# Nineteen identity products on TensorE and five row scalings moved to GpSimd, in the opening of a two-layer kernel

## What is computed

```
mod = silu(c) @ w_ada + b_ada
shift, scale, gate = split(mod, 3)
h = x * rsqrt(mean(x*x) + eps) * norm_gain * (1 + scale) + shift
proj = h @ w_in
```

## Time and profile before

| | us |
|---|---|
| three runs | 1460.65, 1461.0, 1461.27 |
| profiled execution, its time | 1461.91 |
| its span in the trace | 1460.2 |
| TensorE busy | 1436.3 |
| VectorE busy | 741.5 |
| ScalarE busy | 601.3 |
| GpSimd busy | 112.4 |
| mean granted clock of TensorE, share of full | 0.995 |

### The profile page before, as it was taken

The page is one execution under the profiler, slowest core; times in us unless marked ns, Lnnn a source line. Parts: engine busy times, 40 slices in busy tenths (PEclk is TensorE's granted clock), DMA queues, the critical chain, the costliest instruction groups (busy, mean ns, idle before and its releaser), DMA issues.

```text
span 1460.2 us, 18290 instructions
## 1 busy us (share of the span) xinstructions
PE 1436.3 (98%) x6990; PEld 1207.1 (83%) x6990; DVE 741.5 (51%) x1200; ACT 601.3 (41%) x1009; POOL 112.4 (8%) x131
## 2 busy tenths in 40 slices
PE   6999999999999999999999999999999999999998
PEld 5788879998888888888888888888888888888887
DVE  6741677855665533556455444453457333333332
ACT  5633577755343332333333444532355333333221
POOL 5302322210000000000000111100000000000000
PEclk9999999999999999999999999999999999999999
DMA  9995200123433333312223233344332333333321
GB/s 283 322 237 186 75 1 2 31 73 93 152 101 109 98 97 101 101 44 87 68 63 87 58 87 101 87 144 113 89 90 84 115 89 101 99 93 94 110 79 57
DMA packets 227825, 149.71 MB, mean 103 GB/s; under 512 B 5330, under 2 KB 216014, under 8 KB 227108
## 3 DMA queue, kind: packets, MB, share of 16 engines
q1 hardware_dynamic: 223588, 131.63, 31.2%
q0 software_dynamic: 4160, 17.04, 4.0%
HBM read 140.92 MB, written 6.68 MB: 101 GB/s over the span
## 4 chain that ended last, share of the span: by engine, by line
PE 95%; SPq 1%; DMA 1%; DVE 1%; ACT 1%; issue 1%; DVEq 0%; ACTq 0%
PE ps L433 70%; PE ps L2215 6%; PE ps L2241 3%; PE ps L1938 3%; PE ps L2140 3%; PE ps L1830 3%; PE ps L2227 1%; DMA w_raw<-in_w_in_dram 1%; PE ps L1961 1%; PE ps L1899 1%; PE ps L2126 1%; PE ps L2125 1%; SPq L547 1%; PE ps L1954 1%; SPq L577 0%
## 5 line engine op out<-in xcount | busy, mean ns | idle before, releaser
L453 DVE TENSOR_TENSOR w_lo<-w_raw,w_hi 128x1024 fp32r<-128x1024 f32 (+1 forms) x214 | 258.1, 1209 | 251.0 <-ACT w_hi L448 248.1
L448 ACT ACTIVATE w_hi<-w_raw 128x1024 fp32r<-128x1024 f32 (+1 forms) x214 | 219.4, 1034 | 15.3 <-PE ps L433 11.3
L499 ACT ACTIVATE temps<-ps 128x512 f32<-128x512 f32 x67 | 40.0, 597 | 238.9 <-PE ps L433 238.9
L433 PE MATMUL ps<-g_hi,w_hi 128*128 128x512 f32 x384 | 95.8, 392 | 0.0
L433 PE MATMUL ps<-g_hi,w_lo 128*128 128x512 f32 x384 | 94.9, 389 | 0.0
L433 PE MATMUL ps<-g_lo,w_hi 128*128 128x512 f32 x384 | 94.8, 389 | 0.0
L433 PEld LDWEIGHTS ps<-g_hi,w_lo 128*128 128x128 f32 x384 | 72.1, 188 | 15.0
L433 PEld LDWEIGHTS ps<-g_lo,w_hi 128*128 128x128 f32 x384 | 72.1, 188 | 14.9
L433 PEld LDWEIGHTS ps<-g_hi,w_hi 128*128 128x128 f32 x384 | 71.5, 188 | 14.6
L433 PE MATMUL ps<-f_lo,w_hi 128*128 128x512 f32 x288 | 71.1, 389 | 0.0
L433 PE MATMUL ps<-f_hi,w_hi 128*128 128x512 f32 x288 | 71.1, 389 | 0.0
(11 more groups left out here) (442 smaller groups left out, 2734.8 us busy)
## 6 DMA issues: line engine op xcount, KB each, us to landing
w_raw<-in_w_in_dram SPq DMA_DIRECT2D x107, 512.0 KB, 3.9
w_raw<-in_w_ff_gate_dram SPq DMA_DIRECT2D x22, 512.0 KB, 3.8
w_raw<-in_w_ff_up_dram SPq DMA_DIRECT2D x22, 512.0 KB, 3.8
w_ada_shift_scale<-in_w_ada_dram SPq DMA_DIRECT2D x16, 512.0 KB, 7.8
w_raw<-in_w_r_out_dram SPq DMA_DIRECT2D x16, 512.0 KB, 4.5
w_raw<-in_w_ff_down_dram SPq DMA_DIRECT2D x16, 512.0 KB, 4.2
w_ada_gate<-in_w_ada_dram SPq DMA_DIRECT2D x4, 1024.0 KB, 10.9
x_spill<-x_t POOLq DMA_DIRECT2D x2, 2048.0 KB, 9.0
```

The costliest lines, as they stand in the source:

```text
L433: mm = pe.matmul(bank, w[:, slot, k], mov[:, at_k], start=first and n == 0 and k == 0, stop=last and n == 2 and k == kts - 1)
L448: act.activation(whi[:, slot, 0:kts], raw[:, slot, 0:kts], ACT.Copy).then_inc(hi_done, 1)
L453: nc.vector.tensor_tensor(wlo[:, slot, 0:kts], raw[:, slot, 0:kts], whi[:, slot, 0:kts].bitcast(F32), ALU.subtract).then_inc(lo_done, 1)
L499: act.activation(dst, ps[:, o % 4], func, scale=scale).then_inc(evac, 1)
```

## The change

Two things change, both in the opening.

TensorE gets `keep_busy(n)`, which issues n products of the 128x128 identity with itself, in fp32, into the first 128 columns of PSUM bank 0. Nothing reads them, and the first GEMM overwrites them. Fourteen stand between `rows_bc` and `mod_sums(0)`, five between `mod_sums(0)` and the GEMM. Ahead of each group TensorE waits for three copies of x, the third of which frees bank 0.

`x_rstd` for k-tiles 3 to 7 leaves VectorE. GpSimd does them, after it has issued the copy of the bias line; each waits until `xr_done` has reached k, so product 3 waits for VectorE's third, and each later one for the one before it on GpSimd.

```diff
+X_DVE = 3
+BUSY_AT = (14, 5)
@@ GpSimd, after the copy of the bias line
+            pool.wait_ge(m["row_done"], 1)
+            pool.wait_ge(m["x_ev"], X_ACT)
+            pool.wait_ge(m["x_ev2"], KT - X_ACT)
+            for k in range(X_DVE, KT):
+                pool.wait_ge(m["xr_done"], k)
+                g.tensor_tensor(x_r[:, k], x_t[:, k], rs_row[:], ALU.mult).then_inc(m["xr_done"], 1)
             pool.wait_ge(m["ada_done"], KT)
             pool.wait_ge(m["hl_done"], KT)
@@ VectorE, in the loop over u
-                if u < KT - 1:
+                if u + 1 < X_DVE:
                     x_rstd(u + 1)
@@ TensorE, ahead of the first GEMM
+            def keep_busy(n):
+                pe.wait_ge(m["x_ev"], 3)
+                for _ in range(n):
+                    pe.matmul(ps[:, 0, 0:P], ident[:], ident[:], start=True, stop=True)
+
             pe.wait_ge(m["x_ev"], 2)
             pe.wait_ge(m["rms_rs"], 1)
             rows_bc(7).then_inc(m["rms_bc"], 1)
+            keep_busy(BUSY_AT[0])
             mod_sums(0)
+            keep_busy(BUSY_AT[1])
```

## The result

The changed kernel takes 1466.8 us (median of six runs, 1465.5 to 1468.6) against 1461.1 for the one before, run beside it (six runs, 1460.7 to 1462.2). The ratio is 1.0039, 95% interval 1.0028 to 1.0049: 5.7 us slower. The forecast was 1462.6 with a range up to 1466.0. The time lies 0.8 us above the range, on the side of the rival called alternation, which the prediction put at 1465.7, between 1464.4 and 1466.8.

The account below looks back on a forecast made before the run. TensorE, busy 98%, was taken to bound the kernel, with a DMA floor at 44.60 us in the opening. Identity products and freed VectorE gave 0, GpSimd's hold on VectorE +1.6 us: median 1462.6 us, range 1459.9 to 1466.0.

Parts of the forecast that it names:

- alternation: Opening: GpSimd products follow every single VectorE operation, all in before 40 us; +4.7, 1465.7 us (1464.4 to 1466.8), chance 0.31.
- The fill: Identity products on TensorE before the first GEMM: cost 0, clock kept at full speed, step 1 near 27.7, end gain 0.
- the case that the prediction listed last among its rivals: Opening: clock falls despite the identity products, steps 0 to 3 unmoved, end as in another case; no chance of its own.
- The floor: TensorE's step u = 4 is held to 44.60 us by a DMA load, so earlier clock gains end at 0.
- The scalings taken from VectorE: Opening: VectorE loses five operations of 0.60 us that TensorE did not wait for; gain 0.
- The price of a product: Each GpSimd product holds off VectorE operations with two SBUF inputs, costing VectorE up to 1.15 us.
- The sum: Whole forecast effect: +1.6 us, from products held to true gaps in VectorE's queue, other terms 0.
- gap order: Opening: GpSimd gets in only at true gaps between VectorE operations, last product near 52 us; +1.6 us, chance 0.36.
- the two signs named as proof of a wrong prediction: Step 4 starting before 44.4 us, or VectorE's rows keeping their lengths beside GpSimd's products.
- The rival's own sum: For alternation: ada_sum(3) whole at 40.9, TensorE idle 5.4 us, +3.4 at step 4, plus 1.3 for one half-clock pass.
- From the trace to the median: Profiled execution with +1.6 would be 1463.5 us; it ran 0.9 above the median, so 1462.6 was forecast.
- the leak: Opening: a load lands earlier because work ahead of it ended earlier, and step 1's 1.2 us survive; 1459.8 us, chance 0.06.

Follow-up runs that it names:

- kernel 1: Changed kernel with all eight scalings back on VectorE, the 19 identity products kept: 1461.21 us, ratio 0.9998 to the kernel before.
- kernel 9: Changed kernel with all eight scalings on VectorE and only two GpSimd products (k-tiles 3 and 4) that nobody reads: 1462.28 us, 1.0007 against the kernel before.
- 4: Changed kernel with all eight scalings on VectorE and five GpSimd memsets, which read nothing, at the products' place: 1460.99 us, 0.9999 against the kernel before.
- 8: Changed kernel with all scalings on VectorE; ScalarE and VectorE split weight tiles of steps 3 to 6 one step later: 1461.02 us, 0.9998 against the kernel before.
- kernel 7: Changed kernel with the scaling of k-tiles 3 to 7 left out altogether, ScalarE reading the unscaled tile: 1461.28 us, 1.0001 against the kernel before.
- kernel 2: Changed kernel without the identity products, scalings of k-tiles 3 to 7 still on GpSimd: 1466.74 us, 1.0039 against the kernel before.
- kernel 10: Changed kernel with VectorE scaling k-tiles 0 to 5 and GpSimd only 6 and 7: 1464.48 us, 1.0024 against the kernel before.
- 3: Changed kernel with all eight scalings on VectorE and five GpSimd products into a tile nobody reads: 1466.06 us, 1.0035 against the kernel before.
- kernel 5: Changed kernel plus 19 more identity products on TensorE in step 2, ahead of the sums that wait for ada_sum(3): 1464.28 us, 1.0022 against the kernel before.
- kernel 6: Changed kernel with each GpSimd product after the first waiting for its step's ada_sum, one product per step: 1462.67 us, 1.0008 against the kernel before.

## Why the prediction was wrong, point by point

- **The fill, right.** 14 products took 3.29 us, 0.235 each instead of the 0.22 read from products of half as many columns, five took 1.36 to their last end, neither reached what follows, and the clock was 1.00. Its cost is 0 and so is its gain (kernel 1). Step 1 stood at 27.67 for 27.7 foretold, which is partly luck: in the other kernels with the fill it began at 27.5 to 29.0. And in kernel 9 the clock fell in spite of the fill, the case that the prediction listed last among its rivals.
- **The floor, right in its effect, incomplete in its place.** In the four kernels without products on GpSimd (1, 4, 7, 8) step 4 started at 44.23 to 44.82, whatever else was done. It is held by two loads in a row (kernel 8), not by one, and its place differs by 0.6 us among these four traces.
- **The scalings taken from VectorE gain nothing, right** (kernel 7).
- **The price of a product, right.** Up to 1.15 was the bound, 1.02 to 1.05 measured, in after and in kernels 2, 9 and 10. That it is GpSimd's read is shown (3 against 4).
- **The order in which the two engines take turns: the step that failed.** The sum took the gap order, in which GpSimd gets in only where VectorE's queue is truly empty. It gets in after every single instruction of VectorE, whose records overlap: last product at 37.6, not 52; six multiply-adds at 6.55. The prediction held against alternation that no row showed such a moment inside a stream. But a row that is missing speaks for neither side. The row that showed GpSimd waiting, 866.35, had it begin when VectorE's read ended, at a time when VectorE had nothing queued behind it: the next `w_lo` came at 868.13. So it couldn't tell the two orders apart, and no row of before stood for the gap order. It was taken at 0.36 against 0.31, and the +1.6 us of the sum rests on it alone; measured were +4.7 in the trace. Neither of the two signs named as proof of a wrong prediction came, since both were signs against the floor and the price; the sign that told was the start of the last product, near 38 for alternation.
- **The rival's own sum** held up in the trace: `ada_sum(3)` whole at 40.47 (40.9 foretold), 4.53 us idle (5.4), and at step 4 +3.4 for the wait and +1.3 for the clock, 4.7 together, where 4.73 was measured. Its parts were off in opposite ways, 3.0 and 1.8, so that the sum fits better than its parts, by luck; kernel 5 confirms the split, with 3.1 and 1.6.
- **From the trace to the median: the smaller error.** The trace accounts for 4.7 us, the medians differ by 5.7. The prediction took 0.9 off because the profiled execution of before stood above its median; that of after stood 0.7 below its own (1466.11 against 1466.83). The six spans of after go from 1463.8 to 1466.2, and the profiled one is at the lower end. What differs between executions of one kernel is seen in part in the last section. That it makes up this last 1.0 us is not shown, since only one execution of each has a trace. (The lower end of the range, 1459.9, lay 0.1 above the 1459.8 of the leak that it was meant to take in; nothing rests on it.)

What the change did, then: nothing at its first part, and at its second it traded 0.60 us of VectorE for 1.02, five times within 7.5 us. Step 4 starts at 44.60 without it, so step 3 may start as late as 39.66 and `ada_sum(3)` be whole as late as 37.57 (4.94 and 2.09 earlier). It was whole at 35.26, which left a cover of 2.3 us; that took up the two products of kernel 9 (37.76) but for 0.2 (0.35 by its step 4). With five it was whole at 40.47, 2.9 too late, and the clock that the first part had kept up fell in a new place for another 1.6 to 2.6.

## What to carry to other kernels

Where work goes from VectorE to GpSimd and GpSimd reads SBUF beside operations of VectorE with two SBUF inputs, price each GpSimd instruction at most of its length on VectorE's queue, at once, and compare that with what VectorE is rid of (1.02 against 0.60 here). Where a chain of products can be spread, one to a step, the loss falls to a quarter (1.2 against 4.7 in the traces of kernel 6 and of after), but nothing is gained. And where a new wait of TensorE appears, ask what the clock does behind it: in kernel 10 the slow passes cost as much as the wait.

## What the runs showed of the hardware

- **Turns.** VectorE, whose queue was never empty, didn't keep GpSimd out: a waiting GpSimd instruction went ahead of the next instruction of VectorE each time. Six multiply-adds took 2.46 us with no product among them, 3.49 with one (kernel 6), 4.55 with two (kernel 9), 6.55 with four (after) and 7.58 with five (kernel 2). The Trainium skill's rule for this pair ("SBUF — State Buffer", section "Who interferes with whom") is that issue order decides who is blocked. The rows agree as far as they go: they show one instruction each in turn.
- **Half clock came behind a short idle time, but not each time.** Kernel 10 idled 1.49 us at 52 to 53.5, and the clock was 0.50 at 56 to 58. In kernel 9 it fell to 0.60 and 0.55 behind 0.98 and 0.33 us. Idle times of 1.23 us in kernel 1 (ahead of 34.40) and 1.28 us in kernel 7 (ahead of 39.36) were followed by no fall. The prediction had only the pair 3.56 and 1.55 to go by and expected a fall behind more than both. The length of the idle time alone doesn't tell.
- **A second stretch at half clock, far from the change, comes and goes.** In attention, at 224 to 230 us, the profile of before, by stretch:

```profile
224.00:226.00 2.00, 1.75 (x11) 1.61 (x11) 0.85 (x6) 1.65 (x8) 1.08 (x1) 0.75 0.00 0
226.00:228.00 2.00, 2.00 (x12) 2.00 (x12) 1.36 (x6) 1.31 (x5) 0.00 (x0) 0.50 0.00 0
```

and that of after in the same stretch:

```profile
226.00:228.00 2.00, 1.94 (x19) 1.78 (x18) 1.89 (x9) 1.06 (x5) 0.00 (x0) 1.00 0.00 0
```

  Kernels 1 and 4 show it too (0.50 at 226 to 228), and kernel 2, whose opening lost 5.3 us, shows one at 230 to 234 (0.54 and 0.61); the other seven don't. The profiled execution of before had it and that of after hadn't, and across it the distance between the two shrinks: the same exponential on ScalarE starts 4.7 us later in after ahead of it (217.01 against 212.28) and 3.6 behind it (243.50 against 239.86). That is why their spans differ by 3.6 us although the opening alone lost 4.7. What decides about it was not tested.
